# Gate and up products in two PSUM banks, a down product in three column pieces, and waits by matrix in the last quad, in a one-core decoder block on Trainium2

## The reference, cut to what matters

```python
h = (silu(einsum('td,edf->tef', xt, w_gate))
     * einsum('td,edf->tef', xt, w_up)
     * combine[..., None])
y = einsum('tef,efd->td', h, w_down)
x = layer_norm(alpha * x + y, ln2_g, ln2_b)
```

## Time and profile before

| what | us |
|---|---|
| median of 3 runs | 428.95 (427.96 to 429.46) |
| the profiled execution's own time | 429.79 |
| its span in the trace | 427.9 |
| TensorE busy in the span | 376.1 (88%) |
| mean granted TensorE clock | 0.94 of full speed |

### The profile page before, as it was taken

How to read it: one execution, slowest core, us unless ns; L and a number is a source line. 1 busy time by engine, 2 the same in 40 slices (tenths; PEclk the granted TensorE clock), 3 DMA queues, 4 the chain that set the end, 5 groups by cost and what they waited for, 6 DMA issues and landing times.

```text
span 427.9 us, 6989 instructions
## 1 busy us (share of the span) xinstructions
PE 376.1 (88%) x2801; PEld 274.3 (64%) x2801; DVE 158.3 (37%) x330; ACT 131.9 (31%) x225; POOL 29.2 (7%) x40
## 2 busy tenths in 40 slices
PE   8889899999999999998799999489399797595794
PEld 7889898989899999996655454325235244144243
DVE  2444577776355646447512121201200202012026
ACT  4245455735443444418122121201201112011010
POOL 3000000000000000001000026720000000000004
PEclk9999999999999999998799999979779899699698
DMA  8889885746468686899389499999999999999912
GB/s 290 212 309 373 290 283 154 270 136 221 161 180 288 196 292 198 285 414 417 160 319 375 194 367 425 424 417 420 423 419 421 422 422 420 417 424 419 389 60 98
DMA packets 53998, 132.69 MB, mean 310 GB/s; under 512 B 6610, under 2 KB 39378, under 8 KB 42196
## 3 DMA queue, kind: packets, MB, share of 16 engines
q1 hardware_dynamic: 53908, 132.30, 81.7%
q0 software_dynamic: 64, 0.01, 0.0%
HBM read 131.25 MB, written 1.05 MB: 309 GB/s over the span
## 4 chain that ended last, share of the span: by engine, by line
PE 52%; DMA 21%; SPq 12%; DVE 8%; ACT 3%; issue 2%; POOL 1%; POOLq 0%; ACTq 0%; DVEq 0%
PE bank L1017 22%; DMA gu<-in_w_up 19%; PE bank L1246 10%; SPq L361 8%; PE bank L1135 5%; PE bank L1274 4%; PE bank L1112 3%; SPq L393 2%; PE bank L1211 2%; DVE wl L717 2%; DMA raw<-in_w_in 2%; PE bank L1281 1%; SPq L366 1%; ACT wh L566 1%; PE bank L1180 1%
## 5 line engine op out<-in xcount | busy, mean ns | idle before, releaser
L1246 PE MATMUL bank<-gu,xg 128*32 128x512 f32 (+1 forms) x576 | 68.3, 635 | 31.9 <-DMA gu<-in_w_up 31.9
L717 DVE TENSOR_TENSOR wl<-raw,wh 128x1024 fp32r<-128x1024 f32 x56 | 68.4, 1224 | 69.5 <-ACT wh L566 69.2
L1017 PE MATMUL bank<-xh,wh 128*128 128x256 f32 x288 | 83.0, 288 | 3.5 <-ACT qT L611 2.3
L1017 PE MATMUL bank<-xl,wh 128*128 128x256 f32 x288 | 81.5, 283 | 0.0
L1017 PE MATMUL bank<-xh,wl 128*128 128x256 f32 x288 | 81.5, 283 | 0.0
L566 ACT ACTIVATE wh<-raw 128x1024 fp32r<-128x1024 f32 x56 | 58.7, 1055 | 66.3 <-PE bank L1017 31.7
L1246 PEld LDWEIGHTS bank<-gu,xg 128*32 128x32 f32 x576 | 20.7, 123 | 74.6 <-issue 71.7
L1017 PEld LDWEIGHTS bank<-xh,wh 128*128 128x128 f32 x288 | 55.2, 192 | 6.2 <-issue 4.5
L1017 PEld LDWEIGHTS bank<-xl,wh 128*128 128x128 f32 x288 | 55.2, 192 | 0.2 <-issue 0.2
L1017 PEld LDWEIGHTS bank<-xh,wl 128*128 128x128 f32 x288 | 55.2, 192 | 0.0
L1211 PEld LDWEIGHTS bank<-pick,x1p 128*128 128x128 f32 x288 | 35.1, 200 | 5.2 <-issue 3.8
(11 more groups left out here) (197 smaller groups left out, 452.4 us busy)
## 6 DMA issues: line engine op xcount, KB each, us to landing
gu<-in_w_gate SPq DMA_DIRECT2D x32, 1024.0 KB, 21.2
gu<-in_w_up SPq DMA_DIRECT2D x32, 1024.0 KB, 26.0
dn<-in_w_down SPq DMA_DIRECT2D x25, 1024.0 KB, 17.2
raw<-in_w_in SPq DMA_DIRECT2D x40, 512.0 KB, 5.0
raw<-in_w_o SPq DMA_DIRECT2D x8, 512.0 KB, 4.6
dn<-in_w_down SPq DMA_DIRECT2D x8, 512.0 KB, 15.3
raw<-in_w_out_conv SPq DMA_DIRECT2D x4, 512.0 KB, 3.6
raw<-in_w_out_attn SPq DMA_DIRECT2D x4, 512.0 KB, 4.6
```

Of the source, the lines that this page charges most:

```text
L717: dve.tensor_tensor(wl[:, s, :].rearrange("p (k c) -> p k c", k=KC), raw[:, pair % NRAW, :].rearrange("p (k c) -> p k c", k=KC) [:, :, n % ...
L1017: mm = pe.matmul(dst, w[:, k, :], v[:, i, :], start=(i == 0 and w is h and v is high_in), stop=(i == len(ks) - 1 and w is l))
L1246: mm = pe.matmul(bank[6][g, part.start * DE:part.stop * DE], xg[:, k, g], w[:, e, part, k, :], start=(k == 0), stop=(k == KC - 1), skip_gr ...
```

## The change

TensorE computes gate and up apart in every quad, each 256 columns wide: gate into bank 6, up into bank 5. The gate product raises `gate_ps`, on which ACT's sigmoid now waits; DVE's second multiply waits for `gu_ps`. The small products of a round go to bank 4 instead of 5. The down product has three pieces, 512, 256 and 256 columns, in banks 4, 5 and 6; ACT copies pieces 0 and 2, DVE piece 1. In the last quad the first piece is scattered before the last piece's product. There, TensorE waits for each expert's gate matrix by itself, with 12 small products after each of the first three waits, then does the gate product, and the same again for up. The last quad's down weights come in 12 pieces. POOL computes the shift in one instruction.

```diff
+Y_PIECES = ((4, 0, HALF), (5, HALF, HALF + HALF // 2), (6, HALF + HALF // 2, DM))
+NY = len(Y_PIECES)
+WARM_LAST = 12
@@ loads (SP)
-            def load_dn_cols(h, q):
+            def load_dn_cols(i, q):
+                _, lo, hi = Y_PIECES[i]
                 for e in range(QE):
-                    sp.dma_start(dn[:, e, :, h * HALF:(h + 1) * HALF],
-                                 wd_v[:, q * QE + e, :, h * HALF:(h + 1) * HALF]
-                                 ).then_inc(dn_cols_in[h], 16)
+                    sp.dma_start(dn[:, e, :, lo:hi], wd_v[:, q * QE + e, :, lo:hi]).then_inc(dn_cols_in[i], 16)
+            def load_last_gu(c):
+                for e in range(QE):
+                    sp.dma_start(gu[(NQ - 1) % 2][:, e, c, :, :],
+                                 (wg_v, wu_v)[c][:, (NQ - 1) * QE + e, :, :]).then_inc(last_gu_in[c][e], 16)
...
             sp.wait_ge(gu_ps, through(NQ - 2))
-            load_gu((NQ - 1) % 2, NQ - 1)
-            sp.wait_ge(y_ps, 2 * through(NQ - 1))
-            for h in range(2):
-                load_dn_cols(h, NQ - 1)
+            for c in range(2):
+                load_last_gu(c)
+            sp.wait_ge(y_ps, NY * through(NQ - 1))
+            for i in range(NY):
+                load_dn_cols(i, NQ - 1)
@@ POOL
-            link(pool.tensor_tensor(shift[:, 0:1], moments[:, t, 0:1], rstd[:, t:t + 1], ALU.mult))
-            pool.tensor_scalar(shift[:, 0:1], shift[:, 0:1], -1.0, None,
-                               ALU.mult).then_inc(shift_done, 1)
+            pool.tensor_scalar(shift[:, 0:1], moments[:, t, 0:1], rstd[:, t:t + 1], -1.0,
+                               ALU.mult, ALU.mult).then_inc(shift_done, 1)
@@ ACT
-                act.wait_ge(gu_ps, n)
+                act.wait_ge(gate_ps, n)
...
-                act.wait_ge(y_ps, 2 * n - 1)
-                act.activation(ys[:, 0:HALF], bank[4][:, :], ACT.Copy).then_inc(bank_free[4], 1)
+                for i in (0, 2):
+                    b, lo, hi = Y_PIECES[i]
+                    act.wait_ge(y_ps, NY * n - (NY - 1) + i)
+                    act.activation(ys[:, lo:hi], bank[b][:, 0:hi - lo], ACT.Copy).then_inc(y_taken[i], 1)
@@ DVE
-                dve.tensor_tensor(hs[:, :], hs[:, :], bank[6][:, DE:2 * DE],
+                dve.wait_ge(gu_ps, c + 1)
+                dve.tensor_tensor(hs[:, :], hs[:, :], bank[5][:, 0:DE],
                                   ALU.mult).then_inc(bank_free[6], 1)
-                dve.wait_ge(y_ps, 2 * c + 2)
-                dve.tensor_copy(ys[:, HALF:DM], bank[5][:, :]).then_inc(bank_free[5], 1)
+                b, lo, hi = Y_PIECES[1]
+                dve.wait_ge(y_ps, NY * c + 2)
+                dve.tensor_copy(ys[:, lo:hi], bank[b][:, 0:hi - lo]).then_inc(y_taken[1], 1)
...
-            total = dve.value_load(bounds[0:1, NQ:NQ + 1], min_val=NQ, max_val=MAX_ROUNDS)
...
-            dve.wait_ge(added, 4 * total + 2)
+            first = 2 * TT + TT * NY * last
             for t in range(TT):
+                dve.wait_ge(added, first + t + 1)
                 dve.bn_stats(stats[:, t, 0, :], bank[2 * t][:, :])
             for t in range(TT):
-                dve.wait_ge(added, 4 * total + 3 + t)
+                dve.wait_ge(added, first + TT * (NY - 1) + t + 1)
@@ TensorE, quad()
-                        pe.wait_ge(gu_in[half], 2 * QE * 16 * loads)
-                        passes = [slice(0, 1), slice(1, 2)] if q == 0 else [slice(0, 2)]
-                        for part in passes:
+                        if not last_quad:
+                            pe.wait_ge(gu_in[half], 2 * QE * 16 * loads)
+                        for part in range(2):
+                            if last_quad:
+                                pe.wait_ge(bank_free[7], c + 1)
+                                for e in range(QE):
+                                    pe.wait_ge(last_gu_in[part][e], 16)
+                                    if e < QE - 1:
+                                        stay_warm(WARM_LAST)
...
-                                    mm = pe.matmul(bank[6][g, part.start * DE:part.stop * DE], xg[:, k, g],
+                                    mm = pe.matmul(bank[6 - part][g, 0:DE], xg[:, k, g],
...
-                            mm.then_inc(gu_ps if part.stop == 2 else gate_ps, 1)
+                            mm.then_inc(gu_ps if part else gate_ps, 1)
...
+                        down(0)
+                        down(1)
+                        if last_quad:
+                            scatter(0)
+                            down(2)
+                        else:
+                            down(2)
+                            scatter(0)
+                        scatter(1)
+                        scatter(2)
                         gather(c + 1)
```

More of the change, by code:

```diff
@@ L231, in hybrid_block @@
         ln2_done = sem("ln2_done")
-        dn_cols_in = [sem(f"dn_cols_in{i}") for i in range(2)]
+        dn_cols_in = [sem(f"dn_cols_in{i}") for i in range(NY)]
+        last_gu_in = [[sem(f"last_gu_in{c}{e}") for e in range(QE)] for c in range(2)]
         out_done = sem("out_done")
@@ L289, in hybrid_block @@
         bank_free = {b: sem(f"bank_free{b}") for b in (4, 5, 6, 7)}
+        y_taken = [sem(f"y_taken{i}") for i in range(NY)]
         pick_done = sem("pick_done")
@@ L439, in _ @@
             load_gu(0, 2, parts=[0])
-            sp.wait_ge(y_ps, 2 * over)
+            sp.wait_ge(y_ps, NY * over)
             for e in range(NE_EARLY, QE):
@@ L443, in _ @@
             load_gu(0, 2, parts=[1])
-            sp.wait_ge(y_ps, 2 * through(2))
+            sp.wait_ge(y_ps, NY * through(2))
             for i, v in enumerate((ln1_g, ln1_b)):
@@ L452, in load_quad @@
                 load_gu(h, q)
-                sp.wait_ge(y_ps, 2 * through(q))
+                sp.wait_ge(y_ps, NY * through(q))
                 load_dn(q)
@@ L1229, in dn_of, with quad @@
                 return dn_early[e] if q == 1 and e < NE_EARLY else dn[:, e, :, :]
-            def quad(q, first, half, loads, in_columns):
+            def quad(q, first, half, loads, last_quad):
                     w = gu[half]
@@ L1255, in quad @@
                         mm.then_inc(put_ps, 1)
-                        stay_warm(WARM_ROUND[0], 5)
+                        stay_warm(WARM_ROUND[0], 4)
                         pe.wait_ge(bank_free[6], c + 2)
@@ L1262, in quad, with down @@
                         mm.then_inc(hT_ps, 1)
-                        stay_warm(WARM_ROUND[1], 5)
+                        stay_warm(WARM_ROUND[1], 4)
                         pe.wait_ge(bank_free[7], c + 2)
[L1265 to L1269, removed]
+                        def down(i):
+                            b, lo, hi = Y_PIECES[i]
+                            if last_quad:
+                                pe.wait_ge(dn_cols_in[i], QE * 16)
+                            elif i == 0:
                                 dn_loaded(q)
@@ L1273, in quad, with scatter @@
                                     g = slice(SLOTS * e, SLOTS * (e + 1))
-                                    mm = pe.matmul(bank[4 + h][g, :], hT[:, j, g],
-                                                   dn_of(q, e)[:, j, h * HALF:(h + 1) * HALF],
+                                    mm = pe.matmul(bank[b][g, 0:hi - lo], hT[:, j, g], dn_of(q, e)[:, j, lo:hi],
                                                    start=(j == 0), stop=(j == FC - 1))
                             mm.then_inc(y_ps, 1)
-                        for h in range(2):
-                            pe.wait_ge(bank_free[4 + h], c + 2)
+                        def scatter(i):
+                            _, lo, hi = Y_PIECES[i]
+                            pe.wait_ge(y_taken[i], c + 1)
                             for t in range(TT):
-                                pe.matmul(bank[2 * t + h][:, :], put[:, t * P:(t + 1) * P],
-                                          ys[:, h * HALF:(h + 1) * HALF], start=False, stop=True,
+                                pe.matmul(bank[2 * t + lo // HALF][:, lo % HALF:lo % HALF + hi - lo],
+                                          put[:, t * P:(t + 1) * P], ys[:, lo:hi], start=False, stop=True,
                                           skip_group_check=True).then_inc(added, 1)
+                        down(0)
+                        down(1)
+                        if last_quad:
+                            scatter(0)
[5 more added lines that the diff above has]
+                        scatter(2)
                         gather(c + 1)
```

## The result

The changed kernel takes 436.51 us (median of 4 runs, 435.78 to 437.47), the kernel before, measured beside it, 429.2. The ratio is 1.0153, with a 95% interval of 1.0123 to 1.0183: slower by 1.5%. The profiled execution took 435.95 us with a span of 434.2, against 429.79 and 427.9.

What follows compares the result with a forecast made beforehand. Expert weights set the pace, the last up matrix landing at 398.7. Up to the end of the up product +5.75, tail -0.25, sum +5.5; from the median 428.95 this gives 434.45, with a +0.24 clock correction 434.7, range 432.8 to 437.0.

Steps and rivals of the forecast that it cites:

- All gate matrices are in before TensorE is free, and no branch skips the fill.: Last quad: gate matrices land by 388.7, TensorE is free at 391.3; all 72 small products are paid, 16.5 us.
- Split at no cost: Gate and up products apart: 3.5 us each, the pair costing what the joint product costs at full clock, 7.07.
- The clock kept: Last quad: with the small products TensorE never stops, so its product gets back 2.5 us lost to the low clock.
- hs 0.3 sooner a round: Each round: sigmoid and first multiply run beside the up product, taking 0.3 us out before the transposes; net -0.25.
- The up matrices have all landed by 398.2.: Last quad, before the up product: the wait for the up matrices costs nothing.
- rival A: Last quad: the small products run hidden inside the waits, so the kernel gets faster, 422.3 us; chance 0.05.
- Tail -0.25: After the last up product: three terms, -0.3, +0.35 and -0.28, sum to -0.25 us.
- The terms for hs: Tail of the last quad: hs is ready sooner after the up product, -0.3 us.
- scatter order: Tail: the first tile's second half is complete only within the last scatter, delaying its statistics by +0.35, bounds 0 and +0.6.
- shift: Tail, on the chain: POOL's shift is one instruction instead of two, -0.28 us.
- C: Small products run at the low clock level, each costing twice, +16.5 us and more: 451; chance 0.03.
- D: Eight more semaphore waits and two changeovers cost more: +1.5, 436.2, inside the forecast's range; forecast including this 0.90.

## Why the prediction was right

Forecast 434.7 with a range of 432.8 to 437.0, slower with 0.93; measured 436.51. The mechanism was right: the fill, paid in full on TensorE for 16.4 us of which 7.3 had been idle.

- **All gate matrices are in before TensorE is free, and no branch skips the fill.** Right: the chain to the end of the up product was to be +5.75 and was +5.71. The fills and products themselves were right to 0.1 us. That the sum is right to 0.04 is luck: the product of quad 6 began 0.78 us earlier than before, where 0.5 was forecast, and took 9.43 us instead of 9.16, and in the variants of the changed kernel, which share the code up to there, it begins anywhere from 366.9 to 370.4. Fill 8.2 us twice, gate product at 398.8 (measured 398.56), up product at 410.5 (410.38), end at 414.0 (413.97).
- **Split at no cost.** Right: 7.11 us for both parts at full clock, 7.07 before.
- **The clock kept.** Right: 1.00 throughout. The 2.5 us that the clock had cost are confirmed where the fill is free: 9.61 becomes 7.07, and the kernel gains 2.1 us.
- **hs 0.3 sooner a round.** Right, slightly too small: the products of rounds 1 and 2 start 20.00 us apart (231.30 to 251.30), 20.36 before. The half microsecond that this was to bring to the start of the stream can't be seen: that start varies between 243.7 and 248.0 over the profiled executions of all kernels.
- **"The up matrices have all landed by 398.2."** Wrong, by about 1.2 us, and without effect here, as the fill reached to 410.4. The last packet of these matrices ended at 398.8, and the kernels that wait for it start 0.6 us later, so they were in at 399.4. The DMA engines fell silent by 410, not from about 408.5. It would have mattered in rival A, and does in the kernels with less fill. The term that it put at nothing without a reason is the loading of 1531 more instructions.
- **Tail -0.25.** The terms for hs (-0.42 for -0.3), scatter order (+0.43 for +0.35) and shift (-0.24 for -0.28) were right; missing was the collision of VectorE and POOL, +0.82 in the last part. The saved POOL instruction was booked as a gain of 0.28 and cost about 0.6 net.
- **The size.** Between the profiled executions the difference is 6.2 us in time, 0.7 above the sum of 5.5, and the collision explains it. The medians differ by 7.3; the rest is that the profiled execution of before was above its median and that of after below. The forecast started from the median of before and so came 1.8 us short, within its range.
- **Rivals.** A and C did not occur. D, dearer changeovers, did not either: fill and products cost to 0.1 us what the rows said. The part of the range above the forecast, where the time fell, had been meant mainly for D, and was reached by the collision and the spread of executions; the tail's +0.59 lies outside its own bounds (-0.25, give or take 0.3). That the whole stayed inside is in part luck. A's mechanism is real, but needs the fill to be in the gap, as in the kernel with 32 small products there.

## What to carry to other kernels

Fill that keeps TensorE's clock pays only where the engine would have stood idle: compare the time at which it becomes free with each landing, and give the fill the length of that gap, not of a transfer. When a stream of weights sets the pace, count instructions too: 750 more in idle time made the last weights late here, with the fetches as the likely cause. An instruction saved on a chain can move another engine's start ahead of its neighbour's, and the collision can cost more than was saved, as the two instructions of POOL's shift showed.

## What the runs showed of the hardware that was not expected

- 750 more instructions on an engine with time to spare made the last weights of the kernel 1.7 us later (interval 31.50 instead of 29.82), and 1245 to 1317 more 1.3 to 1.6; with 384 more they were not later (29.90). It looks like a step, not like a slope. Each interval is that of one profiled execution.
- A pair of VectorE instructions with two SBUF inputs took 2.42 us instead of 1.42 when a POOL multiply on SBUF had started 0.1 us ahead of the second one.
- 2.87 us of idleness of TensorE in the kernel with 8 down loads were followed by a scatter at the lower clock (3.37 us instead of 1.98); an idle gap of 0.8 us in the kernel with 12 loads was not.
